# Two of eight token blocks by a dense pass over both expert tables, the other six by gathers

## Chip, cores and metric

The kernel runs on one core of a Trainium2 chip, all data in f32. The metric is the device time of one execution in microseconds. The median of three runs counts.

## What is computed

One layer of a decoder for 1024 prompt tokens and 32 sample tokens of width 1024. A token mixer comes first (adaLN, input projection, causal pooling and a convolution over 31 tokens, output projection). Then each token picks experts and adds their outputs:

```python
q = (hf @ w_query).reshape(-1, PEER_HEADS, 2, PEER_HALF)
s = jnp.einsum('nhpk,hpmk->nhpm', q, sub_keys)          # 8 heads, 2 x 128 keys
sv, si = lax.top_k(s, 16)
comb, cidx = ...                                         # 16 x 16 sums, i * 128 + j
fv, fpos = lax.top_k(comb, 16)
eid, gate = ..., jax.nn.softmax(fv)
a = jnp.einsum('phkd,pd->phk', u_table[ex], hx)          # 128 experts of 16384 a token
act = jax.nn.gelu(a) * gx
out = jnp.einsum('phk,phkd->pd', act, v_table[ex])
```

A last gated residual add and a final RMSNorm give the outputs. Both tables have 16384 rows of 4 KB, 67 MB each.

## The kernel before

The 1056 tokens form nine blocks: 0 to 7 of 128 prompt tokens, block 8 (SB) with the 32 sample tokens. For a block of 128 tokens the kernel fetches 128 "u tiles": tile k holds, on partition t, row `eid[t, k]` of u_table (GpSimd's indirect DMA in `u_fetch`, L807, 128 rows of 4 KB). VectorE multiplies it with h2 and sums over the row (L1381), which gives one dot per token. ScalarE applies Gelu (L965), VectorE the gate (`weigh`). Then it fetches 128 "v tiles": tile t holds the 128 rows of v_table that token t picked (`v_fetch`, L827), and TensorE multiplies it with the token's 128 weights into the accumulator banks 0 and 1 (`tokens`, L1758, four tokens in four groups of columns). `finish` adds the residual and norms a block. u tiles land in a ring of six places, v tiles in another of six.

Everything else is written into a table of slots. A slot is one pass of the loop over `p` (block) and `c` (NCH = 32 a block): four u tiles of block p, and from slot 17 on (V_LAG) four v tiles of the tokens 17 slots behind. Every engine walks the slots in order, and after its part of the gathers it does the steps that the slot lists. `lay_out` makes this table: `fill` puts the steps of the token mixer and of the query projection and scores for block groups 1 (blocks 2, 3, 4) and 2 (blocks 5, 6, 7, SB) one after another, each with a TensorE cost from COST, and goes to the next slot when the slot's load is over ROOM (7 for group 1, 4.6 for group 2, 9 in the first sixteen); `("gap", n)` moves on by n slots; two scores stand two slots apart. A score ("s", L1684) is followed by "best", VectorE's top 16 of four heads' keys in two halves (`key_tops`, L1270 to L1278). `spread` places the six pieces ("top", `piece`) by which VectorE makes the 16 x 16 sums, their top 16 and the expert numbers (L1294 to L1342). VectorE does a slot's steps one slot late (DVE_LAG). Group 0 (blocks 0 and 1) is done before slot 0, in the prologue. Weights come in tiles of 1 MB into two places of wring. The queue of SyncE loads and stores x, x1, h2 and y by a list `transfers` that is made from the slots. The steps stand in slots 5 to 184; the table has 288 slots, and the last 32 v tiles come behind it.

## Time and profile before

| | us |
|---|---|
| median of three runs | 3471.02 |
| lowest and highest | 3469.92, 3482.42 |
| span of the profiled execution | 3289.1 |
| TensorE busy | 2159.5 |
| VectorE busy | 2139.4 |
| GpSimd busy | 2280.5 |
| ScalarE busy | 368.6 |

The page gives no time of the profiled execution beside its span, which runs from the first to the last instruction; the runs' time holds what lies around it too. The mean granted clock of TensorE is 0.823 of full speed, 1235 MB are moved at a mean of 376 GB/s. A busy share says how long an engine had an instruction under way, with waits that lie inside an instruction's modelled duration.

### The profile page before, as it was taken

The page shows a single profiled execution, that of the slowest core. Times are in us where ns is not written, and L with a number is a line of the kernel's source. Part 1 is how long each engine was busy: PE and PEld are TensorE (multiplying, and loading weights), DVE is VectorE, ACT ScalarE, POOL GpSimd, SP SyncE. Part 2 cuts the span into 40 slices and gives each one's busy share as a digit, 9 for nine tenths or more (in the row PEclk, how much of TensorE's full clock was granted, in tenths as well). Part 3 has the DMA queues.
Part 4 walks back from the last instruction along what each step waited for, and adds up shares of the span by engine and source line. Part 5 has one row for each costly group of instructions (what it writes and reads, how often), then busy time and mean ns, then how long its engine had stood idle before and what let it go on. Part 6 is the DMA issues. An engine that isn't in the chain of part 4 may idle for free.

```text
span 3289.1 us, 30699 instructions
## 1 busy us (share of the span) xinstructions
PE 2159.5 (66%) x9831; PEld 958.8 (29%) x9831; DVE 2139.4 (65%) x4892; ACT 368.6 (11%) x793; POOL 2280.5 (69%) x2229
## 2 busy tenths in 40 slices
PE   6885896756776468997855577767454445545556
PEld 5573442212443113453211143434111111111111
DVE  1577756676788855666575657877766666677431
ACT  2112231100010110222100100001000000000000
POOL 0144677776777777777776777777777777777765
PEclk9997998977887789999877688889767777667679
DMA  8778899999999999999999999999999999999998
GB/s 290 202 273 299 326 385 386 388 401 401 397 395 389 360 396 406 405 405 386 382 400 394 375 399 390 392 382 370 369 405 406 402 402 406 406 385 402 382 363 321
DMA packets 363454, 1235.08 MB, mean 376 GB/s; under 512 B 36855, under 2 KB 40335, under 8 KB 363279
## 3 DMA queue, kind: packets, MB, share of 16 engines
q0 software_dynamic: 304784, 1109.40, 87.4%
q1 hardware_dynamic: 36335, 79.69, 6.8%
q10 hardware_dynamic: 22176, 44.04, 3.6%
q8 instruction: 79, 1.29, 0.2%
q14 instruction: 80, 0.66, 0.1%
HBM read 1220.31 MB, written 13.28 MB: 375 GB/s over the span
## 4 chain that ended last, share of the span: by engine, by line
POOL 29%; DMA 27%; PE 24%; issue 11%; DVE 7%; DVEq 1%; ACT 1%; SPq 0%; POOLq 0%; ACTq 0%
DMA v_ring<-in_v_table_dram,eidt 21%; POOL u_ring L807 15%; POOL v_ring L827 14%; PE bank L1758 13%; DMA u_ring<-in_u_table_dram,eid 4%; PE bank L1586 3%; PE bank L1668 2%; DVE u_ring L1381 2%; PE bank L1569 2%; PE bank L1644 2%; DMA u_ring<-in_v_table_dram,eidt 1%; DVE mixt L1211 1%; DVE work L1272 0%; DMA u_ring<-in_w_ada_dram 0%; POOL u_ring L827 0%
## 5 line engine op out<-in xcount | busy, mean ns | idle before, releaser
L1758 PE MATMUL bank<-v_ring,act_x 128*32 128x512 f32 x4104 | 1177.7, 808 | 977.7 <-DMA v_ring<-in_v_table_dram,eidt 929.9
L1381 DVE CUSTOM_DVE_ANT_0 u_ring<-u_ring,h 128x1024 f32<-128x1024 f32 x1056 | 1279.5, 1226 | 785.4 <-DMA u_ring<-in_u_table_dram,eid 711.9
L807 POOL DMA_INDIRECT u_ring<-in_u_table_dram,eid x1024 | 1129.9, 1103 | 444.0 <-issue 312.2
L827 POOL DMA_INDIRECT v_ring<-in_v_table_dram,eidt x1026 | 1070.3, 1043 | 397.3 <-issue 245.8
L1758 PEld LDWEIGHTS bank<-v_ring,act_x 128*32 128x32 f32 x4104 | 271.4, 135 | 1794.3 <-issue 1785.0
L1668 PEld LDWEIGHTS bank<-hbuf,wring 128*128 128x128 f32 x1984 | 228.4, 194 | 22.0 <-issue 22.0
L1668 PE MATMUL bank<-hbuf,wring 128*128 128x128 f32 (+1 forms) x1984 | 234.4, 279 | 0.0
L1586 PE MATMUL bank<-zc,dring 128*128 128x384 f32 x496 | 193.3, 514 | 4.0 <-ACT dring L860 4.0
L1569 PE MATMUL bank<-hbuf,wring 128*128 128x384 f32 (+2 forms) x448 | 150.8, 495 | 22.7 <-DMA wring<-in_w_in_dram 13.7
L1644 PE MATMUL bank<-wring,mixt 128*128 128x512 f32 (+1 forms) x256 | 123.2, 631 | 0.0
L1569 PEld LDWEIGHTS bank<-hbuf,wring 128*128 128x128 f32 x448 | 85.7, 194 | 89.7 <-issue 50.8
L1586 PEld LDWEIGHTS bank<-zc,dring 128*128 128x128 f32 x496 | 84.3, 192 | 58.0 <-issue 21.6
L860 ACT ACTIVATE dring<-ident,cw 128x128 f32<-128x128 f32 x248 | 78.1, 389 | 124.6 <-PE bank L1588 75.0
L1381 DVE DVE_READ_ACCUMULATOR2_ANT dot<- 128x1 f32 x1056 | 87.0, 82 | 0.0
L1409 DVE TENSOR_TENSOR scratch<-bank,mod 128x512 f32<-128x512 f32 x18 | 11.6, 686 | 102.1 <-PE bank L1758 100.8
L965 ACT ACTIVATE dot<-dot 128x32 f32<-128x32 f32 x33 | 7.6, 229 | 627.5 <-DVE dot L1381 627.4
L1644 PEld LDWEIGHTS bank<-wring,mixt 128*128 128x128 f32 (+1 forms) x256 | 46.7, 190 | 77.5 <-issue 77.5
L955 ACT ACT_TABLE_LOAD x34 | 43.6, 1283 | 144.4 <-PE bank L1644 95.5
L944 ACT ACTIVATE qt<-bank 128x512 f32<-128x512 f32 (+1 forms) x36 | 20.2, 561 | 350.1 <-PE bank L1668 350.1
L1588 PEld LDWEIGHTS bank<-zcs,dring 128*128 128x128 f32 x248 | 46.9, 189 | 33.0
L786 POOL DMA_DIRECT2D hbuf<-in_b_out_dram x1 | 0.7, 696 | 79.0 <-PE bank L1569 79.0
L1301 DVE TENSOR_TENSOR work<-fhalff,iota 128x512 f32<-128x512 f32 x72 | 49.8, 692 | 7.6 <-issue 0.7
(267 smaller groups left out, 1696.6 us busy)
## 6 DMA issues: line engine op xcount, KB each, us to landing
v_ring<-in_v_table_dram,eidt POOLq DMA_INDIRECT x1026, 6.9
u_ring<-in_u_table_dram,eid POOLq DMA_INDIRECT x1024, 6.8
wring<-in_w_out_dram ACTq DMA_DIRECT2D x16, 1024.0 KB, 11.9
wring<-in_w_query_dram ACTq DMA_DIRECT2D x16, 1024.0 KB, 11.7
wring<-in_w_in_dram ACTq DMA_DIRECT2D x10, 1024.0 KB, 11.8
xr<-in_x_prompt_dram SPq DMA_DIRECT2D x16, 512.0 KB, 7.4
v_ring<-in_w_ada_dram SPq DMA_DIRECT2D x7, 1024.0 KB, 13.4
wring<-in_w_ada_dram SPq DMA_DIRECT2D x5, 1024.0 KB, 5.6
```

The source lines that it names most:

```text
L807: pool.indirect_dma_start(u_ring[:, n % NU], None, u_table[0], bass.IndirectOffsetOnAxis(ap=col, axis=0)).then_inc(u_in[n % NU], 16)
L827: pool.indirect_dma_start(place, None, v_table[0], bass.IndirectOffsetOnAxis(ap=eidt[:, b % RING, t:t + 1], axis=0)).then_inc(landed, 16)
L860: last = act.activation(diag_at(g, c, j), ident[:, :], ACT.Copy, scale=cw[:, j, c:c + 1])
L955: act.activation(g, g, ACT.Exp).then_inc(exp_ready, 1)
L1301: dve.tensor_tensor(hot[:, :, :, :], fhalff[:, :, a * K:(a + 1) * K].unsqueeze(3).broadcast_to(shape), iota[:, :].unsqueeze(1).unsqueeze(1 ...
L1381: dve.tensor_tensor_reduce(u_ring[:, n % NU], u_ring[:, n % NU], h2[:, b % 2], 1.0, 0.0, ALU.mult, ALU.add, dot[:, b % 2, k:k + 1]).then_i ...
L1569: last = pe.matmul(ps[PROJ[c]][:, 0:n], w[:, k, c * P:(c + 1) * P], h1t[:, h * HK + k, 0:n], start=(h + k == 0), stop=(h * HK + k == KC - 1))
L1586: last = pe.matmul(ps[2 + c % 2][:, 0:np], diag_at(g, c, j), zc[:, c, j:j + np], start=(j == 0), stop=(j == CK - 1))
L1588: last = pe.matmul(ps[7][:, c * S:(c + 1) * S], diag_at(g, c, j), zcs[:, c, :, j:j + TS], start=(j == 0), stop=(j == CK - 1))
L1644: last = pe.matmul(bank, mixt[:, h * HK + k, t0:t0 + n], w[:, k, :], start=False, stop=(h * HK + k == KC - 1))
L1668: last = pe.matmul(q_bank(b)[:, a * n:(a + 1) * n], w[:, k, a * P:(a + 1) * P], h2_cols(b)[:, h * HK + k, :], start=(h + a + k == 0), stop ...
L1758: last = pe.matmul(acc[h][j * S:(j + 1) * S, :], act_x[:, i % 2, j, a:a + S], v_place(n)[0][:, h * HALF:(h + 1) * HALF], start=(c == 0), s ...
```

## The change

Blocks 2 and 3 no longer gather. Seven positions (POS: blocks 0, 1, 4, 5, 6, 7, SB) go through the slots, so the table has 224 slots. For the pair (2, 3), 256 tokens, the selection keeps the two key numbers and the gate of each pick (`dn`), and three new kinds of step follow in the slots.

- "numbers" and "unit": TensorE turns gates and key numbers. For four tokens at a time VectorE makes the first keys' one-hot times gate (`first_keys`: four comparisons over 128 columns), ScalarE the second keys' one-hot (`second_keys`: four Abs over 128 columns and one Relu over 512), TensorE multiplies them into a 128 x 128 gate matrix per token, ScalarE copies 512 columns out, and SyncE stores 16 tokens at a time in pieces of 512 bytes to `g_dram` (16.8 MB in all).
- "round" m: table tile m of u (128 experts, 512 KB) is turned by eight transposes, tile m - 3 is multiplied with the 256 tokens' h2 (eight products of 256 columns), ScalarE applies Gelu, VectorE multiplies with the gates loaded from `g_dram`, and four products of 512 columns with tile m - 6 of v add to banks 2 to 5. There are 134 rounds with 128 of each kind of work (130 transposed tiles, two of them h2 itself).
- two more ends (`finish`) for the dense blocks.

The new planner gives more room a slot (12 and 13), gaps are shorter, scores stand one slot apart, and VectorE does "best" in the slot of the score. The planner's text gives: mixer, query and score steps in slots 5 to 97; units six a slot in slots 98 to 108; rounds two a slot in 109 to 175, one round after each pair of tokens; gathers alone from 176. The v ring has five places, the sixth holds `dn` and constants. Tiles of u and v of the tables are loaded by SyncE's queue, three and five rounds ahead, into places that the mixer used. DVE, ACT and PE do a slot's dense steps between their parts of the gathers.

```diff
@@ -41,7 +41,7 @@
...
-NV = 6
+NV = 5
...
 PASSES = [[bs[i:i + 2] for i in range(0, len(bs), 2)] for bs in GROUPS]
-ROOM = [None, 7, 4.6]
+ROOM = [None, 12, 13]
+POS = [0, 1, 4, 5, 6, 7, SB]
+NPP = len(POS) - 1
+POS_OF = {b: p for p, b in enumerate(POS)}
+NSLOT = (NPP + 1) * NCH
+DENSE = [[2, 3]]
+DENSE_OF = {b: (r, q) for r, bs in enumerate(DENSE) for q, b in enumerate(bs)}
+NDB = 2
+DT = NDB * P
+NTILE = NKEY + NDB
+W_LAG = 4
+VD_LAG = 6
+NROUND = NKEY + VD_LAG
+UNIT = 4
+NUNIT = DT // UNIT
+STOK = 16
+NSTAGE = DT // STOK
+IC = 8
+NCHUNK = NKEY // IC
+NUD, NVD, NGE = 4, 6, 4
 MAXP = 3 * P
@@ -177,7 +196,7 @@
                 at = max(at, last + i[1])
                 continue
             if i[0] == "s":
-                at = max(at, scored.get("last", 0) + 2)
+                at = max(at, scored.get("last", 0) + 1)
             while load[at] >= (9 if at < LAG else room):
@@ -187,9 +206,9 @@
...
-                scored["last"], scored[i[1:]] = at, at + 1
+                scored["last"], scored[i[1:]] = at, at
                 for h in range(2):
-                    slots[at + h].append(("best", *i[1:], h))
+                    slots[at].append(("best", *i[1:], h))
         return at
@@ -224,9 +243,48 @@
...
-    for b in range(1, NB + 1):
-        last = spread(top_steps([(part, b) for part in range(PARTS)]), max(last, 24 + 30 * (b - 1)), min(24 + 30 * b, NB * NCH - 3))
+    for b, (s0, s1) in TOP_SLOTS.items():
...
+TOP_SLOTS = {1: (20, 30), 2: (36, 47), 3: (47, 57), 4: (55, 72), 5: (80, 96), 6: (98, 122), 7: (122, 152), SB: (152, NSLOT - NCH - 4)}
+GEN_UNITS, ROUNDS = (6,), (2,)
+
...
+def lay_out_dense(steps):
+
+    slots = [[] for _ in range(NSLOT)]
+    pieces = {"exp", "nrm", "top", "turn", "turned"}
+    at = max(s for s, todo in enumerate(steps) if any(x[0] not in pieces for x in todo)) + 2
+    ends = []
+    for r, bs in enumerate(DENSE):
+        at = max(at, max(s for s, todo in enumerate(steps) if ("nrm", PARTS - 1, bs[-1]) in todo) + 2)
+        slots[at] += [("numbers", r, q) for q in range(NDB)]
+        for u in range(NUNIT):
+            slots[at + u // GEN_UNITS[r]].append(("unit", r, u))
+        at += (NUNIT - 1) // GEN_UNITS[r] + 1
+        slots[at].append(("last", r))
+        for m in range(NROUND):
+            slots[at + m // ROUNDS[r]].append(("round", r, m))
+        at += (NROUND - 1) // ROUNDS[r] + 1
+        ends.append(at)
+    return slots, ends
+
+
...
+    g_dram = [nc.dram_tensor(f"gates_scratch{r}", [NDB, NCHUNK, P, P // STOK, IC, STOK], F32, kind="Internal").ap() for r in range(len(DENSE))]
...
+        gij = mflat[:, 0:6 * P].rearrange("p (q x t) -> p q x t", q=NDB, x=3)
...
+        zcf, zpf, zcsf = (z.rearrange(r) for z, r in ((zc[:, :, :], "p g n -> p (g n)"), (zp[:, :, :], "p g n -> p (g n)"),
+                                                      (zcs[:, :, :, :], "p g b n -> p (g b n)")))
+        oh_i, oh_j = (z[:, 0:2 * UNIT * P].rearrange("p (r t e) -> p r t e", r=2, t=UNIT) for z in (zcf, zpf))
+        ht = keyt[:, :, :].rearrange("p a m -> p (a m)").rearrange("p (k t) -> p k t", k=KC)
+        ut = [hbuf[:, i * D:(i + 1) * D] for i in range(2)]
+        ge = hbuf[:, 2 * D:3 * D].rearrange("p (r t) -> p r t", r=NGE)
+        gch = [wring[:, i].rearrange("p k n -> p (k n)").rearrange("p (b t i c) -> p b t i c", b=NDB, t=P // STOK, i=IC) for i in range(2)]
+        ud = [xr[:, 0], xr[:, 1], gt1[:, :], qt[:, :, :, :].rearrange("p i a n -> p (i a n)")]
+        vd = [mod2[:, 0], mod2[:, 1], dring[:, :, :].rearrange("p i k -> p (i k)"), zcf[:, 0:D], zpf[:, 0:D], zcsf[:, 0:D]]
         act_x = sb("act_x", [P, 2, 4, XW])
@@ -610,20 +718,101 @@
...
+            def stage_store(r, k):
+
+                n = r * NSTAGE + k
+                sp.wait_ge(unit_taken, (n + 1) * (STOK // UNIT))
+                q, t = divmod(k, P // STOK)
+                sp.dma_start(g_dram[r][q, :, :, t].rearrange("c j i t -> j c (i t)"),
+                             stage[n % 2].rearrange("p (c i) t -> p c (i t)", i=IC)).then_inc(g_stored[n % 2], 16)
...
+            def ud_load(r, t):
+
+                n = r * NTILE + t
+                if n >= NUD:
+                    sp.wait_ge(ut_ps, 2 * (n - NUD) + 2)
...
+                    sp.wait_ge(h2_stored[b % 2], 16 * (b // 2))
+                    src = h2_dram[b]
+                else:
+                    src = u_table[0, (t - NDB) * P:(t - NDB + 1) * P, :]
...
+            def vd_load(r, i):
+
+                n = r * NKEY + i
+                if n >= NVD:
...
+                    sp.wait_ge(st_ps, 4)
+                sp.dma_start(vd[n % NVD], v_table[0, i * P:(i + 1) * P, :]).then_inc(vd_in[n % NVD], 16)
...
+            def g_load(r, c):
+
+                n = r * NCHUNK + c
+                if n >= 2:
+                    sp.wait_ge(wd_ready, IC * (n - 1))
...
+                        sp.wait_ge(g_stored[a], 16 * NSTAGE // 2 * (r + 1))
+                sp.dma_start(gch[n % 2].rearrange("p b t i c -> p b (t i c)"),
+                             g_dram[r][:, c].rearrange("b j t i c -> j b (t i c)")).then_inc(g_in[n % 2], 16)
@@ -992,6 +1185,81 @@
...
+            def second_keys(r, u):
...
+                    act.wait_ge(unit_ps, n - 1)
+                for i in range(UNIT):
+                    act.activation(oh_j[:, n % 2, i], iota_e, ACT.Abs, bias=gij[:, q, 2, t + i:t + i + 1])
+                if u:
+                    unit_out(r, u - 1)
+                act.drain()
+                act.activation(oh_j[:, n % 2], oh_j[:, n % 2], ACT.Relu, bias=one_c, scale=-1.0).then_inc(oh_j_ready, 1)
...
+            def unit_out(r, u):
...
+                act.activation(stage[k % 2][:, :, i * UNIT:(i + 1) * UNIT].rearrange("p i t -> p t i"),
+                               ps[2 + n % 4][:, :].rearrange("p (t i) -> p t i", t=UNIT), ACT.Copy).then_inc(unit_taken, 1)
...
+            def dense_round(r, m):
+
+                if m < NTILE:
+                    n = r * NTILE + m
+                    for h in range(2):
+                        act.wait_ge(ut_ps, 2 * n + h + 1)
...
+                        to = ht[:, 4 * h:4 * h + 4, m * P:(m + 1) * P] if m < NDB else ut[m % 2][:, h * HALF:(h + 1) * HALF].rearrange("p (a t) -> p a t", a=4)
+                        act.activation(to, ps[7][:, :].rearrange("p (a t) -> p a t", a=4), ACT.Copy).then_inc(ut_ready, 1)
...
+                if 0 <= i < NKEY:
+                    n = r * NKEY + i
+                    act.wait_ge(a_ps, n + 1)
+                    if n >= NGE:
+                        act.wait_ge(vd_ps, NDB * (n - NGE + 1))
+                    act.activation(ge[:, n % NGE], ps[6][:, DT:2 * DT], ACT.Gelu).then_inc(ge_ready, 1)
@@ -1370,20 +1649,58 @@
...
+            def first_keys(r, u):
...
+                    dve.wait_ge(unit_ps, n - 1)
+                for i in range(UNIT):
+                    last = dve.tensor_scalar(oh_i[:, n % 2, i], iota_e, gij[:, q, 1, t + i:t + i + 1], gij[:, q, 0, t + i:t + i + 1],
+                                             ALU.is_equal, ALU.mult)
+                last.then_inc(oh_i_ready, 1)
...
+            def dense_weights(r, m):
...
+                    n, c = r * NKEY + i, r * NCHUNK + i // IC
+                    dve.wait_ge(ge_ready, n + 1)
+                    if i % IC == 0:
+                        dve.wait_ge(g_in[c % 2], 16 * (c // 2 + 1))
+                    w = ge[:, n % NGE].rearrange("p (a t) -> p a t", t=STOK)
+                    dve.tensor_tensor(w, w, gch[c % 2].rearrange("p b t i c -> p (b t) i c")[:, :, i % IC], ALU.mult).then_inc(wd_ready, 1)
@@ -1453,12 +1785,18 @@
...
                 for c in range(NCH):
-                    if p < NB or c < NSG:
-                        chunk(p, c)
-                    slot = p * NCH + c - DVE_LAG
-                    for step in steps[slot] if slot >= 0 else []:
+                    todo = dense[p * NCH + c]
+                    for end in ends[p * NCH + c]:
+                        finish(end)
+                    for j in range(CH):
+                        if p < NPP or c < NSG:
+                            dots(p, c, j, j + 1)
@@ -1725,29 +2064,115 @@
...
+            def unit(r, u):
...
+                for i in range(UNIT):
+                    last = pe.matmul(ps[2 + n % 4][:, i * P:(i + 1) * P], oh_j[:, n % 2, i], oh_i[:, n % 2, i], start=True, stop=True)
+                last.then_inc(unit_ps, 1)
...
+            def tile_turned(n, h):
...
+                for a in range(4):
+                    last = pe.transpose(ps[7][:, a * P:(a + 1) * P], ud[n % NUD][:, (4 * h + a) * P:(4 * h + a + 1) * P], ident[:, :])
+                last.then_inc(ut_ps, 1)
...
+            def dense_values(r, i, q):
...
+                    pe.wait_ge(vd_in[n % NVD], 16 * (n // NVD + 1))
+                    pe.wait_ge(wd_ready, n + 1)
...
+                for h in range(2):
+                    last = pe.matmul(ps[2 + 2 * q + h][:, :], ge[:, n % NGE, q * P:(q + 1) * P], vd[n % NVD][:, h * HALF:(h + 1) * HALF],
+                                     start=(i == 0), stop=(i == NKEY - 1))
+                last.then_inc(vd_ps, 1)
...
+            def dense_dots(r, i, s):
...
+                    pe.wait_ge(ge_ready, n)
+                for k in range(KC):
+                    last = pe.matmul(ps[6][:, DT:2 * DT], ut[i % 2][:, k * P:(k + 1) * P], ht[:, k, :], start=(k == 0), stop=(k == KC - 1))
+                last.then_inc(a_ps, 1)
...
+            def dense_round(r, m, s):
+
+                for h in range(2):
+                    if m < NTILE:
+                        tile_turned(r * NTILE + m, h)
+                    if 0 <= m - VD_LAG < NKEY:
+                        dense_values(r, m - VD_LAG, h)
+                if 0 <= m - NDB - 1 < NKEY:
+                    dense_dots(r, m - NDB - 1, s)
@@ -1814,15 +2239,22 @@
...
+                        weights(NPP, 0, p * NCH + c)
                     if v_chunk(p * NCH + c):
                         b, vc = v_chunk(p * NCH + c)
                         if vc % LAG == 0:
-                            weights(b, vc // LAG)
-                        tokens(b, vc)
-                    if p == NB and c == NSG + 2:
-                        weights(NB, 0)
+                            weights(b, vc // LAG, p * NCH + c)
+                        tokens(b, vc, (0,))
+                        for step in todo[:len(todo) // 2]:
+                            dense_step(p * NCH + c, *step)
+                        tokens(b, vc, (2,))
```

## Rows read from the trace of the kernel before

**Rows 1.** The page's span, busy times and transfer rate in 40 slices of the span

```profile
span 3289.1 us, 30699 instructions
...
PE 2159.5 (66%) x9831; PEld 958.8 (29%) x9831; DVE 2139.4 (65%) x4892; ACT 368.6 (11%) x793; POOL 2280.5 (69%) x2229
...
GB/s 290 202 273 299 326 385 386 388 401 401 397 395 389 360 396 406 405 405 386 382 400 394 375 399 390 392 382 370 369 405 406 402 402 406 406 385 402 382 363 321
```

**Rows 2.** The page's chain that ended last, by line

```profile
DMA v_ring<-in_v_table_dram,eidt 21%; POOL u_ring L807 15%; POOL v_ring L827 14%; PE bank L1758 13%; DMA u_ring<-in_u_table_dram,eid 4%; PE bank L1586 3%; PE bank L1668 2%; DVE u_ring L1381 2%; PE bank L1569 2%; PE bank L1644 2%; DMA u_ring<-in_v_table_dram,eidt 1%; DVE mixt L1211 1%; DVE work L1272 0%; DMA u_ring<-in_w_ada_dram 0%; POOL u_ring L827 0%
```

**Rows 3.** The page's costliest groups: busy, mean ns of one, idle before and its releaser

```profile
L1758 PE MATMUL bank<-v_ring,act_x 128*32 128x512 f32 x4104 | 1177.7, 808 | 977.7 <-DMA v_ring<-in_v_table_dram,eidt 929.9
L1381 DVE CUSTOM_DVE_ANT_0 u_ring<-u_ring,h 128x1024 f32<-128x1024 f32 x1056 | 1279.5, 1226 | 785.4 <-DMA u_ring<-in_u_table_dram,eid 711.9
```

**Rows 4.** TensorE's timeline near the end: start, duration, one pair of tokens a line

```profile
3208.98 1.91 PE L1758 MATMUL bank<-u_ring,act_x 128*32 128x512 f32 x8 [0.66 <-DMA u_ring<-in_v_table_dram,eidt]
3211.54 1.91 PE L1758 MATMUL bank<-v_ring,act_x 128*32 128x512 f32 x8 [0.65 <-DMA v_ring<-in_v_table_dram,eidt]
```

**Rows 5.** GpSimd's timeline, two gathers in a row

```profile
1337.71 0.93 POOL L807 DMA_INDIRECT u_ring<-in_u_table_dram,eid  x1 [0.30 <-issue]
...
1338.95 0.94 POOL L827 DMA_INDIRECT v_ring<-in_v_table_dram,eidt  x1 [0.30 <-issue]
```

**Rows 6.** Windows: us, busy of PE, PEld, DVE, ACT, POOL, then clock, DMA share, GB/s

```profile
204.90:1329.00 1124.10, 784.23 (x3536) 379.57 (x3536) 804.64 (x1954) 156.53 (x340) 801.56 (x718) 0.85 0.99 380
1329.00:2322.20 993.20, 714.81 (x3398) 338.73 (x3398) 684.56 (x1595) 125.26 (x278) 746.97 (x687) 0.85 1.00 389
2322.20:3079.00 756.80, 384.13 (x1212) 89.93 (x1206) 506.46 (x1043) 39.86 (x68) 572.65 (x570) 0.71 1.02 400
3079.00:3289.10 210.10, 116.29 (x425) 27.67 (x423) 56.11 (x98) 4.43 (x13) 132.48 (x134) 0.84 0.92 346
```

**Rows 7.** Window of slots 0 to 183, the dots' line alone

```profile
204.90:2322.20 2117.30, 892.10 (x1472) 0.85 1.00 384
```

**Rows 8.** VectorE's timeline, two key selections begin

```profile
1960.18 0.29 DVE L1270 MAX8 s_mem<-dring 128x8 f32<-128x128 f32 x1
...
1962.04 0.29 DVE L1270 MAX8 s_mem<-dring 128x8 f32<-128x128 f32 x1
```

**Rows 9.** VectorE's groups by form

```profile
L1304 DVE TENSOR_TENSOR work<-work,sif 128x512 f32<-128x512 f32 x72 | 50.1, 696 | 5.7 <-issue 0.4
...
L1275 DVE MAX8 fv<-work 128x8 f32<-128x256 f32 x72 | 30.8, 428 | 5.3
...
L1144 DVE TENSOR_SCALAR xr<-xr,sst 128x1024 f32<-128x1024 f32 x8 | 6.1, 762 | 0.6
```

**Rows 10.** ScalarE: four 128-column activations in the timeline, and a copy's group

```profile
1482.67 1.28 ACT L860 ACTIVATE dring<-ident,cw 128x128 f32<-128x128 f32 x4 [2.98 <-PE bank L1588]
...
L950 ACT ACTIVATE dring<-bank 128x512 f32<-128x512 f32 x28 | 16.7, 597 | 313.9 <-PE bank L1684 245.5 <-PE bank L1687 68.4
```

**Rows 11.** TensorE's timeline: bursts without waits, and one handover; records counted

```profile
59.47 13.98 PE L1569 MATMUL bank<-hbuf,wring 128*128 128x256 f32 x64
...
148.45 7.13 PE L1644 MATMUL bank<-v_ring,mixt 128*128 128x512 f32 x16
...
183.02 7.31 PE L1668 MATMUL bank<-hbuf,wring 128*128 128x128 f32 x64
191.01 1.16 PE L1684 MATMUL bank<-keyt,qt 128*128 128x128 f32 x8 [0.69 <-ACT qt L944]
...
717.97 1.97 PE L1654 MATMUL bank<-ident,xr 128*128 128x128 f32 x16
...
1509.39 1.94 PE L1758 MATMUL bank<-v_ring,act_x 128*32 128x512 f32 x16
```

**Rows 12.** DMA issues: count, KB each, median us to landing

```profile
wring<-in_w_in_dram ACTq DMA_DIRECT2D x10, 1024.0 KB, 11.8
...
mod_scratch<-y POOLq DMA_DIRECT2D x6, 64.0 KB, 6.4
```

447 lines of the change are left out of this document (338 added, 109 removed).

## Prediction

> **What bounds the kernel now.** I read the page from the top: span and busy shares, then the slices, the chain, the costliest groups, then windows cut at slot boundaries, then single bursts. No engine is busy over 69%, but the transfer rate stands near 400 GB/s in nearly every slice after the eighth [rows 1], and the chain that ended last goes through the gathers of v_ring and GpSimd's issues [rows 2]. TensorE's token product and VectorE's dots lie idle 930 and 712 us waiting for gathered tiles [rows 3]. So the kernel is bound by its 2112 gathers of 0.524 MB. Two details decide about the change. In steady state a pair of v tiles (1.05 MB) comes every 2.56 us [rows 4], 409 GB/s; and GpSimd needs about 1.24 us from issue to issue [rows 5], so the eight gathers of a slot take at least 9.9 us whatever the transfers do. Time taken off the transfers is no use beyond that.
>
> The profiled execution has a span of 3289.1 us, and the median of the runs is 3471.0 us, 181.9 us above it. I sum against the span and add the difference to the median. A measurement of this kernel can tell about 0.5% (17 us) from no change.
>
> **The plan before and after.** A slot is four u tiles and four v tiles. Slot 0 begins at 204.9 us; the before's slot 98 begins at 1328 and its slot 184, where the last mixer and query steps end, at 2322 us [rows 6]. From the planner's text, before: mixer and queries of groups 1 and 2 in slots 5 to 184. After: the same work in slots 5 to 97 (room 12 and 13 against 7 and 4.6, scores one slot apart, VectorE without its lag); slots 98 to 108 build the gate matrix (64 units, six a slot); slots 109 to 175 hold the 134 dense rounds, two a slot; then gathers alone. So there are five stages.
>
> **Prologue, 205 us.** Nothing of it is changed [rows 6].
>
> **Stage A, slots 0 to 97, forecast 1420 us.** Removed nothing, only packed. VectorE was busy 804.6 + 684.6 = 1489 us in the before's slots 0 to 183 [rows 6], 892 us of that in the dots [rows 7]: 1.212 us each for 736. The other 597 us now fall into 98 slots beside 392 dots (475 us): 1072 us busy. Small operations that follow on each other have gaps, which busy time leaves out; I allow a tenth, an estimate, so 597 becomes 657 and VectorE 1132 us. One key selection, gaps included, is 1.86 us from start to start [rows 8]. Transfers: 427.1 + 386.4 = 814 MB in that stretch [rows 6], less 86 slots of gathers (361 MB), is 453 MB, 1132 us at 400 GB/s. Two resources at 1132 us each would overlap perfectly only if both were even, and they are not. Slots 35 to 46 hold twelve scores (48 key selections, 89 us), 48 dots (58 us) and block 2's four parts of pair selection and key numbers: each has six operations over 512 columns at 0.69 us and twelve over 256 columns at 0.42 [rows 9], 9.2 us, 41 us for four with gaps; 188 us or 15.7 us a slot against 11.7 us of transfers. In slots 57 to 61 three convolution steps a slot do the same to TensorE. I priced every step of both plans in this way and took per slot the dearest of VectorE, TensorE and transfers. For the before's slots 0 to 183 that gives 2093 us against 2117 measured, so it may be trusted to some per cent. For the after's 0 to 97 it gives 1430 us; taking the dearest over eight slots together (as if the rings could average that far) it gives 1288 us. The rings hold six and five tiles, little over one slot, so I take 1420. Bounds: 1290, and 1560 if scores stall (below). The before needed 1124 us for these 98 slots [rows 6].
>
> **Stage B, slots 98 to 108, forecast 175 us.** ScalarE builds the second one-hot: per unit four 128x128 activations (1.28 us), one Relu over 128x512 and one 128x512 copy out of PSUM, 0.597 us each [rows 10], and a drain: 2.6 us, 64 times 166 us, plus the turn of the gates. VectorE's four comparisons over 128 columns lie between nothing and the 0.76 us of one over 1024 columns [rows 9]; I take 0.25, near the small end as 128 columns are an eighth of it, so 1 us a unit beside ScalarE. TensorE's four products, 0.228 us each [rows 11], are covered too. The gate matrix, 16.8 MB, is stored in 512-byte pieces. No row has such a store of 1 MB; 64 KB of 512-byte rows land in 6.4 us and 1 MB of 2 KB rows in 11.8 us [rows 12]. Sixteen stores at 11.8 us are 189 us, mostly under ScalarE's time: upper bound 200. The lower bound is the transfers alone, 88 gathers and the matrix, 63 MB, 155 us. The Trainium skill, DMA: Bandwidth & Descriptors, Specifications, puts the smallest transfer for line rate at 512 bytes; by it the store would cost no more than its bytes and the stage would end at ScalarE's 166 us. No row of this trace shows it.
>
> **Stage C, slots 109 to 175, forecast 1275 us.** Here the bound moves to TensorE. Per round it turns one u tile, multiplies it with 256 tokens and multiplies a v tile for two blocks: eight transposes, eight f32 products with 256 columns, four with 512. From back-to-back bursts [rows 11], where an f32 product is two records and a transpose is one: 32 products of 256 columns take 13.98 us (0.437 each), eight of 512 columns 7.13 us (0.89), sixteen transposes 1.97 us (0.123). A round is 3.50 + 3.56 + 0.98 = 8.04 us; less 0.1 us for the drains that end each burst 7.95 us, 128 rounds 1018 us. The token pairs of the gathered blocks are now issued in two halves with a round between them. Four tokens in one go take 1.94 us, a pair alone 1.91 [rows 4, 11], so splitting doubles their price: 134 x 1.91 = 256 us. Sum 1274 us, 19 us a slot. Beside it: transfers, 67 slots of 8 gathers, 4 dense tiles and an eighth of a 2.1 MB gate chunk, 6.55 MB or 16.4 us a slot at 400 GB/s, 1100 us; GpSimd 9.9 us; VectorE 4.85 us of dots, about 1 us of weights and up to 6 us of selections; ScalarE four copies at 0.6 and two Gelu, about 3.5 us. All are hidden by TensorE; if TensorE were free, transfers would be next at 1100. The lags (weights four rounds, values six) leave a round of slack, so the semaphores should cost little. Upper bound: one handover of 0.69 us [rows 11] in each round adds 88 us, with other work 1400. Lower: 1250, since a pair's 1.91 us holds the last product's drain. What the change buys here is the 536 gathers that pass meanwhile, which would take 714 us by themselves; it pays nearly as much again for the rest.
>
> **Stage D, slot 176 to the end, forecast 370 us.** 96 u and 164 v gathers are left. The last 210.1 us of the before [rows 6] moved 35 + 104 = 139; the other 121 are 63.4 MB, 159 us at 400 GB/s. Bounds 350 to 380. The dense blocks' own ends (four multiplications more on VectorE) hide under gathers.
>
> **Sum.** 205 + 1420 + 175 + 1275 + 370 = 3445 us, 156 above 3289, so 3471 + 156 = 3627; I say 3625 us. As a check by differences: 512 gathers saved are 64 slots of 10.66 us (756.8 over 71 plain slots [rows 6]), 682 us, and 86 slots are relieved of mixer work (11.55 to 10.66 us, 77 us); against this stage A is 296 us longer than before, stage B 58 above eleven plain slots, stage C 561 above 67 plain ones. The change moves 8% fewer bytes, but hands the bound to TensorE for 67 slots and to VectorE for much of the first 98.
>
> **Rivals.** *The packed stage averages out, and the change is faster.* If the rings absorb the peaks, stage A is 1290, B 165, C 1250 and D 355: 3265 us, a time of 3447. For it: the transfers alone would allow A in 1132. Against: the before's own slots 160 to 183, where VectorE's part is largest, follow the slot-by-slot sum and not the average. It decides where A and C together fall below 2540 us (forecast 2695). *No change*: the same, half as strong, with A near 1310 and C at 1275, about 3471 to 3515, a narrow case. *Scores stall.* VectorE now selects from a score in the slot in which TensorE makes it: query halves of 3.65 us (16 products at 0.228), two ScalarE copies and the score lie ahead of it, and VectorE's next dots, so GpSimd's next u gather, wait behind it. With 7 us lost in some 20 of the slots 35 to 46 and 80 to 96, A becomes 1560 and the time 3765. For it: the lag and gap that covered this are gone. Against: TensorE runs ahead of VectorE when VectorE is the late one. *Dense rounds starve*: if rounds wait for a table tile or a handover each, C is 1400 or more, time 3750. *The change does not do what it says*, for instance gathers run on and dense rounds trail behind: excluded by the order, each slot's pairs and rounds being written in one program order on TensorE.
>
> **How the numbers follow.** Forecast as summed, 3540 to 3700: 0.50. Scores stall 0.16, rounds starve 0.09: both slower. Faster rival 0.15. No change 0.10. So faster 0.15, same 0.10, slower 0.75. The range runs from 3440 (most of the faster rival and a tenth outside with the mishaps combined) to 3770, which takes in each single upper bound.
>
> **What would show it.** In the profile after: TensorE near full in the stretch of the dense rounds, at a granted clock near 1.0, with 16 dense records of 256 columns a round in about 3.5 us, and the transfer rate there below 360 GB/s; slots of about 19 us (dots per stretch). ScalarE near full for some 170 us before it. In the first 98 slots VectorE busy above 75% and the transfer rate below that of before. Slot 98 should begin near 1625 us, the rounds near 1800, and end near 3075. I am wrong if slot 98 begins by 1500, if the transfer rate stays at 400 in the dense stretch, or if a round takes less than 7.5 us of TensorE.

## The result, and the profile after

| | forecast | measured |
|---|---|---|
| time, median (kernel before beside it: 3470.5) | 3625 (3440 to 3770) | 3775.2 |
| ratio to the kernel before | 1.045 | 1.087, interval 1.083 to 1.091 |
| prologue | 205 | 206.0 |
| stage A, slots 0 to 97 | 1420 | 1607.8 |
| stage B, slots 98 to 108 | 175 | 254.9 |
| stage C, slots 109 to 175 | 1275 | 1295.9 |
| stage D, slot 176 to the end | 370 | 397.6 |

The kernel is slower, as forecast, but by 305 us instead of 154, and the time lies 5 us above the upper end of the range. The profiled execution has a span of 3762.2 us. The stages begin where the first dot of their first slot begins. Slower was right, stage C and the prologue were near (stage C 21 us over), A and B were not: they are 188 and 80 us longer than forecast.

The page of the changed kernel, busy tenths, clock and GB/s in 40 slices (94 us each), and its costliest groups:

```profile
span 3762.2 us, 38955 instructions
...
PE 2910.5 (77%) x13405; PEld 1627.7 (43%) x13405; DVE 1918.9 (51%) x4745; ACT 741.9 (20%) x1532; POOL 1812.7 (48%) x1717
...
PE   7868874665599765765566899999999999984456
...
DVE  2586577578744454677556343333343333346431
...
PEclk9988997887799887877677899999999999997778
DMA  8697688777975799776687998988989898879998
GB/s 282 178 346 248 218 320 306 290 265 257 331 262 186 247 367 354 274 256 219 237 267 252 372 350 321 362 327 332 339 327 350 328 342 332 329 284 380 370 346 314
...
PE bank L2183 12%; PE bank L2144 12%; PE bank L2131 11%; DMA v_ring<-in_v_table_dram,eidt 6%; PE bank L1922 5%; POOL u_ring L999 4%; PE bank L2004 4%; PE bank L2117 3%; POOL v_ring L1020 3%; DVE u_ring L1660 3%; PE bank L1905 3%; PE bank L2107 2%; PE bank L1980 2%; DMA u_ring<-in_u_table_dram,eid 2%
...
L2183 PE MATMUL bank<-v_ring,act_x 128*32 128x512 f32 x3080 | 819.1, 725 | 570.3 <-DMA v_ring<-in_v_table_dram,eidt 519.3
L1660 DVE CUSTOM_DVE_ANT_0 u_ring<-u_ring,h 128x1024 f32<-128x1024 f32 x800 | 950.5, 1223 | 249.0 <-DMA u_ring<-in_u_table_dram,eid 171.0
L2144 PE MATMUL bank<-keyt,hbuf 128*128 128x256 f32 x2048 | 465.8, 381 | 0.0
...
L2107 PE MATMUL bank<-zc,zp 128*128 128x128 f32 x512 | 98.4, 351 | 86.0 <-DVE zc L1675 63.1
```

Against [rows 1] the even 400 GB/s is gone. In slices 3 to 22, which are stages A and B, the rate lies mostly between 180 and 350, and no engine is near full in its place, but for TensorE in slices 12 and 13 (the convolution of blocks 5 to SB). In slices 24 to 35, stage C, TensorE is at 9 with the clock at 0.9 or more, and the rate lies near 340. The chain that ended last no longer goes mainly through gathers as in [rows 2]; its first three entries are products of TensorE. Windows at the stages' bounds, columns as in [rows 6]:

```profile
206.00:1813.80 1607.80, 1115.51 (x5560) 631.38 (x5560) 1045.19 (x2849) 251.61 (x566) 833.26 (x717) 0.84 0.78 280
1813.80:2068.70 254.90, 161.26 (x686) 95.28 (x686) 147.51 (x421) 189.53 (x390) 96.69 (x91) 0.73 0.76 252
2068.70:3364.60 1295.90, 1269.01 (x5206) 730.57 (x5207) 478.27 (x992) 243.34 (x452) 587.09 (x532) 0.99 0.89 335
3364.60:3762.20 397.60, 204.16 (x686) 47.34 (x684) 159.91 (x281) 14.90 (x30) 268.51 (x257) 0.78 0.95 353
```

In A VectorE was busy 1045 us (forecast 1072) and TensorE 1116 of 1608: the work is as counted, the overlap is not. VectorE's share is 65%, where the prediction wanted to see over 75%. In B no engine is busy over three quarters, though ScalarE should have been full. In C TensorE is at 98%.

**One thing about the baseline.** The kernel before took 3294 to 3298 us in two of the batches below and 3464 to 3486 in the others. Its profiled execution, with the span of 3289.1, is one of the first sort. A program's time is some 2 us above its span, so the 181.9 us that the prediction added to the span do not lie around it. What differs is the transfer rate. Slots 192 to 239 of the kernel before hold gathers and a few pieces of the selection, and so they do in p_room, a variant of it below: 10.47 us a slot at 404 GB/s in the first trace, 11.53 us at 366 GB/s in p_room's (windows: us, busy, clock, DMA share, GB/s):

```profile
2411.80:2914.40 502.60, 260.26 (x798) 60.41 (x796) 323.20 (x640) 25.17 (x44) 383.65 (x385) 0.71 1.02 404
```

```profile
2724.00:3277.70 553.70, 269.90 (x798) 58.70 (x796) 321.17 (x636) 23.77 (x42) 396.62 (x386) 0.71 0.97 366
```

The texts written ahead of the runs speak of a chip with 402 and one with 361 GB/s. The record has the same chip number (15) beside both rates; what sets the rate no run shows. Here the two are called the higher and the lower rate.

A kernel bound by transfers feels this, the changed one hardly: stages A to C of the changed kernel took 3159 us at the lower rate and 3141 at the higher one (b_act1, whose edit moved nothing). So the change's price depends on the rate: 8.7% at the lower one; at the higher one the variants b_act1 and b_dve1, both with the stages of the changed kernel, took 3742 and 3758, 13.5 and 14% above 3298. Below, each stage is compared at its own rate. b_ring3, b_act1, b_dve1, c_halfdots, c_unsplit, p_room and nodense ran once each.

### The profile page after: what moved, and what is told of

It reads as the page before. It is cut to its first block, busy times and chain, and to the rows that moved or that the text cites. A ratio compares the mean times of both kernels' runs of the same rounds, so it can differ in the third digit from the quotient of the medians.

```text
span 3762.2 us, 38955 instructions
## 1 busy us (share of the span) xinstructions
PE 2910.5 (77%) x13405; PEld 1627.7 (43%) x13405; DVE 1918.9 (51%) x4745; ACT 741.9 (20%) x1532; POOL 1812.7 (48%) x1717
## 4 chain that ended last, share of the span: by engine, by line
PE 57%; DVE 12%; DMA 10%; issue 8%; POOL 7%; ACT 2%; DVEq 2%; another core or an unknown queue 2%; SPq 0%; ACTq 0%; POOLq 0%
PE bank L2183 12%; PE bank L2144 12%; PE bank L2131 11%; DMA v_ring<-in_v_table_dram,eidt 6%; PE bank L1922 5%; POOL u_ring L999 4%; PE bank L2004 4%; PE bank L2117 3%; POOL v_ring L1020 3%; DVE u_ring L1660 3%; PE bank L1905 3%; PE bank L2107 2%; PE bank L1980 2%; DMA u_ring<-in_u_table_dram,eid 2%
## 5 line engine op out<-in xcount | busy, mean ns | idle before, releaser
L1020 POOL DMA_INDIRECT v_ring<-in_v_table_dram,eidt x770 | 836.7, 1087 | 994.4 <-PE bank L2183 804.2
L999 POOL DMA_INDIRECT u_ring<-in_u_table_dram,eid x768 | 893.9, 1164 | 785.5 <-DVE dot L1660 513.7
L2183 PE MATMUL bank<-v_ring,act_x 128*32 128x512 f32 x3080 | 819.1, 725 | 570.3 <-DMA v_ring<-in_v_table_dram,eidt 519.3
L1660 DVE CUSTOM_DVE_ANT_0 u_ring<-u_ring,h 128x1024 f32<-128x1024 f32 x800 | 950.5, 1223 | 249.0 <-DMA u_ring<-in_u_table_dram,eid 171.0
L2183 PEld LDWEIGHTS bank<-v_ring,act_x 128*32 128x32 f32 x3080 | 173.9, 125 | 1057.7 <-issue 1044.5
L2144 PE MATMUL bank<-keyt,hbuf 128*128 128x256 f32 x2048 | 465.8, 381 | 0.0
L2144 PEld LDWEIGHTS bank<-keyt,hbuf 128*128 128x128 f32 x2048 | 391.1, 191 | 106.9 <-issue 59.8
L1244 ACT ACTIVATE hbuf<-bank 128x512 f32<-128x512 f32 x256 | 152.9, 597 | 458.8 <-PE bank L2117 423.6
L1922 PE MATMUL bank<-zc,dring 128*128 128x384 f32 x496 | 202.9, 536 | 18.9 <-ACT dring L1053 16.8
L2131 PE MATMUL bank<-mod,hbuf 128*128 128x512 f32 x352 | 165.5, 593 | 0.0
L2107 PE MATMUL bank<-zc,zp 128*128 128x128 f32 x512 | 98.4, 351 | 86.0 <-DVE zc L1675 63.1
L1905 PE MATMUL bank<-hbuf,wring 128*128 128x384 f32 (+2 forms) x448 | 150.6, 498 | 16.8 <-DMA wring<-in_w_in_dram 12.6
L1675 DVE TENSOR_SCALAR zc<-v_ring,mixt 128x128 f32<-128x128 f32 x256 | 76.7, 370 | 102.3 <-PE bank L2107 79.3
```

What stands on the lines that cost most here:

```text
L999: pool.indirect_dma_start(u_ring[:, n % NU], None, u_table[0], bass.IndirectOffsetOnAxis(ap=col, axis=0)).then_inc(u_in[n % NU], 16)
L1020: pool.indirect_dma_start(place, None, v_table[0], bass.IndirectOffsetOnAxis(ap=eidt[:, b % RING, t:t + 1], axis=0)).then_inc(landed, 16)
L1660: dve.tensor_tensor_reduce(u_ring[:, n % NU], u_ring[:, n % NU], h2[:, b % 2], 1.0, 0.0, ALU.mult, ALU.add, dot[:, b % 2, k:k + 1]).then_i ...
L1905: last = pe.matmul(ps[PROJ[c]][:, 0:n], w[:, k, c * P:(c + 1) * P], h1t[:, h * HK + k, 0:n], start=(h + k == 0), stop=(h * HK + k == KC - 1))
L1922: last = pe.matmul(ps[2 + c % 2][:, 0:np], diag_at(g, c, j), zc[:, c, j:j + np], start=(j == 0), stop=(j == CK - 1))
L2107: last = pe.matmul(ps[2 + n % 4][:, i * P:(i + 1) * P], oh_j[:, n % 2, i], oh_i[:, n % 2, i], start=True, stop=True)
```

## Experiments

### What sets the first 98 slots

**a_lag**: VectorE does the steps of slots 0 to 96 one slot late, as the kernel before does.

```diff
+LAG_TO = 97
...
-                    for step in steps[p * NCH + c]:
+                    s = p * NCH + c
+                    for step in (steps[s - 1] if 0 < s <= LAG_TO else []) + (steps[s] if s >= LAG_TO else []):
```

> The changed kernel with VectorE doing the steps of slots 0 to 96 one slot late again; nothing else. Theory coupling (in stage A VectorE waits some 330 us for TensorE and ScalarE in the same slot, which the lag had covered): VectorE's waits on them fall below 100 us, slots 0 to 97 take 1430 to 1500 us against 1608, and the kernel 3600 to 3680. Rival (the stage is set by uneven work and small rings alone): stage A stays within 40 us of 1608.

3666.0 us, at the higher rate (3294.5 for the kernel before). Stage A took 1504.4 us, just above the expected 1430 to 1500; the five variants with A untouched took 1591 to 1598 at the same rate. The lag is worth 86 to 94 us (the texts written ahead of the later runs say 103, which compares two rates). VectorE's waits in stage A (source, us in total, times, longest), the changed kernel and then a_lag:

```profile
DVE u_ring L1660 <- DMA u_ring<-in_u_table_dram,eid: 113.8, 54, 11.9
DVE eidt L1639 <- PE bank L2039: 76.5, 5, 34.7
DVE s_mem L1540 <- ACT dring L1143: 37.2, 6, 12.5
DVE tops L1540 <- issue: 29.4, 3, 24.6
DVE fsum L1622 <- ACT gate L1148: 26.4, 2, 24.4
DVE mixt L1494 <- PE bank L1952: 23.9, 2, 20.4
```

```profile
DVE u_ring L1661 <- DMA u_ring<-in_u_table_dram,eid: 226.1, 75, 16.8
DVE eidt L1640 <- PE bank L2041: 45.3, 5, 16.8
DVE zc L1448 <- PE bank L1907: 27.4, 6, 11.2
```

All waits of VectorE except those for gathers fall together from 361 to 138 us (the kernel before: 25 us over slots 0 to 183); those with TensorE or ScalarE as the releaser are 269 and 119 of it. The waits for gathers rise from 114 to 226. VectorE waited for TensorE's turned numbers, for scores and for sums in the very slot in which they are made. How such a wait or a long selection travels, from the changed kernel's timeline (start, duration, idle before and its releaser):

```profile
716.67 0.30 DVE L1540 MAX8 tops<-dring 128x8 f32<-128x128 f32 x1 [24.56 <-issue]
...
724.29 1.23 DVE L1660 CUSTOM_DVE_ANT_0 u_ring<-u_ring,h 128x1024 f32<-128x1024 f32 x1 [0.21 <-issue]
...
725.79 1.68 POOL L999 DMA_INDIRECT u_ring<-in_u_table_dram,eid  x1 [9.47 <-DVE dot L1660]
...
730.07 0.94 POOL L1020 DMA_INDIRECT v_ring<-in_v_table_dram,eidt  x1 [0.30 <-issue]
...
737.60 5.13 PE L2183 MATMUL bank<-v_ring,act_x 128*32 128x512 f32 x16 [15.38 <-DMA v_ring<-in_v_table_dram,eidt]
```

VectorE had stood 24.6 us until a score was there (ScalarE's copy of it ends at 716.6; the profile names no releaser) and then made selections until 724. GpSimd stood 9.5 us at a u gather until a dot freed its place; the v gathers queued behind it started after 730; TensorE idled 15.4 us for them, from 722.2 on, and was then late with its own steps, for which VectorE waits next. The places of the v ring had been free since TensorE's last product of tokens, which ended at 721.1, so some 8 of the 15.4 us passed before the first v gather was issued at all. Over slots 0 to 97 GpSimd stood 405.9 us at u gathers for VectorE's dots, with the lag 235.9, in the kernel before 56.1; TensorE stood 350.0, 257.3 and 259.9 us for v tiles.

**a_mix**: a_lag, and GpSimd issues one u and one v gather in turn.

```diff
                             u_fetch(p, c * CH + j)
-                    if v_chunk(p * NCH + c):
-                        b, vc = v_chunk(p * NCH + c)
-                        for j in range(CH):
+                        if v_chunk(p * NCH + c):
+                            b, vc = v_chunk(p * NCH + c)
                             v_fetch(b, vc * CH + j)
```

> a_lag, and GpSimd issues a slot's gathers in turn, one of u and one of v, instead of four and four. If GpSimd's one queue is the link that still costs (a u gather that waits for VectorE holds back v gathers whose places are free, and the other way round), the first 98 slots fall from 1504 by 20 to 60 us. If the slot-by-slot sum of busy work is what is left, they stay within 10 us.

3729.8 us beside 3486.0; stage A 1562.8 us against 1518.8 for mended2, whose stage A is a_lag's, at the same rate: 44 us longer instead of 20 to 60 shorter. So the order in GpSimd's queue does matter, but this order is worse, and it is not the remedy. Why was not settled; one reading is that a v gather in front of the second u gather can stop the queue for TensorE as well.

**p_room**: the kernel before with the new planner's room alone (longer gaps, lag, six v places and scores two apart stay).

```diff
-ROOM = [None, 7, 4.6]
+ROOM = [None, 12, 13]
```

> The kernel before with only the planner's room changed to 12 and 13, gaps and lag as they were; all eight blocks gather. Theory (packing mixer work costs time of its own, since slots then fall to VectorE or TensorE and the gathers' lead is lost): the kernel is slower than before by 60 to 150 us although nothing is added. Rival (packing is free, the later slots give back what the first lose): within 25 us of before.

3676.4 us beside 3463.8: 213 us, 6.1%, for packing and nothing else, far above the expected 60 to 150. This kernel has no dense work, moves the same bytes and keeps the lag; its mixer and query steps end in slot 147 instead of 184. The late slots do not pay the loss back: slots 152 to 239 took 11.46 us each, the time of their gathers at this rate (slots 192 to 239 have a DMA share of 0.97, above), whatever their engines do not have to do. Where the loss arises is seen best in the sixteen convolution steps of blocks 5 to SB. They stand one a slot in the kernel before (slots 99 to 114) and three a slot here (82 to 87). Windows of these slots in the kernel before and in p_room:

```profile
1341.40:1510.50 169.10, 161.97 (x750) 88.08 (x750) 116.05 (x219) 51.24 (x149) 130.66 (x127) 1.00 1.02 404
```

```profile
1260.00:1379.20 119.20, 114.77 (x510) 70.71 (x509) 42.50 (x78) 35.70 (x109) 48.47 (x48) 0.98 0.66 234
```

One a slot, TensorE (96% busy) and the transfers (404 GB/s) work side by side. Three a slot, TensorE is as full (96%), but the transfers stand at 234 GB/s, and the gathers of ten slots are still to come, 115 us. 119 + 115 is 234 us for what would take some 187 at this rate (169.1 us, at 366 instead of 404 GB/s; an estimate). The work is the same, but it has less beside it.

**nodense**: the changed kernel without numbers, units and rounds (blocks 2 and 3 get no experts).

```diff
-        slots[at] += [("numbers", r, q) for q in range(NDB)]
-        for u in range(NUNIT):
-            slots[at + u // GEN_UNITS[r]].append(("unit", r, u))
...
-        for m in range(NROUND):
-            slots[at + m // ROUNDS[r]].append(("round", r, m))
```

The ends of blocks 2 and 3 wait for the scores and the state here instead of the rounds.

> The gate matrix and all dense rounds are left out, so the outputs of blocks 2 and 3 lack their experts. Theory (stage A does not depend on them, the rest is what the dense pass costs): slots 0 to 97 stay at 1590 to 1610, slots 98 to 175 fall from 1551 to 78 plain slots of about 10.7, 835, and the kernel to about 3030. Rival (the smaller v ring slows plain slots too): slots 98 to 175 take over 880.

3124.2 us; A 1607.3 (unchanged: nothing of the dense part reaches into A), slots 98 to 108 125.7 and 109 to 175 781.8. Together that is 907.5 us, in the range that the text gave to its rival, the smaller v ring. But this batch ran at the lower rate: 78 slots at the 11.5 us of p_room, which has six v places, are 897, so some 10 us at most are left for the ring here. In the changed kernel of the same batch (a0_after) the two stretches are 256.3 and 1300.2: the dense pass costs 131 + 518 = 649 us. It replaces 64 slots of 11.5 us, 736 us, at this rate. By this estimate it gains 87 us by itself; packing the mixer's work ahead of it costs more.

**a0_after** is the changed kernel in that batch.

> The changed kernel, unchanged, beside before on one chip. In the run before this batch the kernel before took 3294 us and not 3471, with the same trace as the one first shown. Theory (the two chips differ in what transfers cost, and only the transfer-bound kernel feels it): if before takes about 3294 here, the changed kernel takes 3740 to 3765, nearly as on the other chip, ratio 1.135 to 1.145. Rival (both scale alike): about 3580, ratio 1.087.

3771.0 us beside 3463.8, ratio 1.088 (1.081 to 1.096): the first result again. This batch ran at the lower rate too, so it could not decide between the two theories; b_act1 and b_dve1, at the higher rate, did: 13.5 and 14% above the kernel before, as the first theory says.

**b0_before** is the kernel before in the batch of a_lag.

> The kernel before, unchanged, for a trace of the same chip as the others. Its profiled span was 3289 us while its runs took 3471. Theory 1 (the shown trace was an execution with quicker transfers than the timed ones): the span is now 3460 to 3480, the prologue about 205, and the missing 180 us are spread over the slots, about 11.9 us a plain slot against 10.66. Theory 2 (some constant lies outside the span): the span is again near 3290.

3295.0 us, span 3286.2, ratio 1.000: its slots follow the first trace's within 3 us.

### What sets a unit's 4 us

**b_ring3**: three one-hot buffers in place of two (`n % 2` becomes `n % 3` for `oh_i` and `oh_j`, and both engines wait for unit n - 3 only).

> Three one-hot buffers instead of two. Theory (the units are slow because VectorE and TensorE hand two buffers back and forth, 79 and 63 us of waits): slots 98 to 108 fall from 255 to 200 to 215. Rival (VectorE's and TensorE's own work in a slot and the token pairs between the units set it): they fall by less than 15 us.

Stage B 253.0 us against 256.3, time 3777.7: no effect.

**b_gen4**: `GEN_UNITS = (4,)` in place of 6.

> The gate matrix is built four units a slot: 16 slots (98 to 113) in place of 11, everything else the same, the rounds begin five slots later. If a unit has a price of its own (about 4 us from one to the next, a chain over ScalarE, VectorE and TensorE), the units end after the same 255 us with five more slots of gathers in them, the last stage is shorter by five plain slots, and the time falls by about 55 us. If slots and units add up (11.5 us a slot and 1.95 us a unit), the 16 slots take 16 x 11.5 + 64 x 1.95 = 309 us and the time stays within 10 us.

Slots 98 to 113 took 258.4 us and the time is 3698.0, 44 us below b_act1 of the same batch. The 64 units have a price of their own, 4.0 us each with the turn of the gates ahead of them, whether 11 or 16 slots of gathers pass beside them.

**b_act1** and **b_dve1**: one operation over 512 columns in place of four over 128, on ScalarE and on VectorE (three of four tokens' numbers are left out).

```diff
-                for i in range(UNIT):
-                    act.activation(oh_j[:, n % 2, i], iota_e, ACT.Abs, bias=gij[:, q, 2, t + i:t + i + 1])
+                act.activation(oh_j[:, n % 2], iota_e.unsqueeze(1).broadcast_to([P, UNIT, P]), ACT.Abs, bias=gij[:, q, 2, t:t + 1])
```

> Slots 98 to 108 with ScalarE's four Abs over 128 columns a unit (1.28 us) made one over 512 columns (about 0.6 us): the key numbers of three of four tokens are left out of the second one-hot. If ScalarE sets the unit's pace, as predicted, the stage falls by up to 64 x 0.7 = 45 us, from 255 to 210. If VectorE's order (comparisons of 1.48 us a unit between its dots, and the dots behind them) sets it, the stage stays within 10 us of 255.

> Slots 98 to 108 with VectorE's four comparisons over 128 columns a unit (1.48 us) made one over 512 columns (about 0.7 us): the key numbers and gates of three of four tokens are left out of the first one-hot. If VectorE is in the loop that sets the pace (comparison, product, copy, and the dots that wait behind them), the stage falls by 30 to 50 us, from 255 to 205 to 225. If ScalarE alone sets it, it stays within 10 us of 255.

Stage B 254.6 and 253.0 us. Neither the Abs nor the comparisons are on the path. The stores hardly are either: in b_act1 a 1 MB store in 512-byte rows lands in 9 us, and one is due every 16:

```profile
gates_scratch<-mixt SPq DMA_DIRECT2D x8, 1024.0 KB, 9.4
gates_scratch<-mod SPq DMA_DIRECT2D x8, 1024.0 KB, 8.7
```

Buffers, Abs and comparisons were out by a run, the stores by their times. The timeline of the changed kernel showed what was left, two units of it:

```profile
1906.29 1.11 DVE L1675 TENSOR_SCALAR zc<-v_ring,mixt 128x128 f32<-128x128 f32 x4 [1.15 <-PE bank L2107]
...
1907.39 0.72 ACT L1216 ACTIVATE zp<-zp,v_ring 128x512 f32<-128x512 f32 x1
1908.02 1.26 ACT L1212 ACTIVATE zp<-v_ring,mixt 128x128 f32<-128x128 f32 x4
...
1908.22 2.04 PE L2107 MATMUL bank<-zc,zp 128*128 128x128 f32 x8 [1.97 <-DVE zc L1675]
...
1910.30 1.04 ACT L1227 ACTIVATE mod<-bank 128x512 f32<-128x512 f32 x1 [1.01 <-PE bank L2107]
...
1911.42 0.72 ACT L1216 ACTIVATE zp<-zp,v_ring 128x512 f32<-128x512 f32 x1
```

The Relu (L1216) ends at 1908.1 and the product begins 0.1 us later. The profile names VectorE's comparison (L1675) as the product's releaser, but that one had ended at 1907.40; in all 64 units of this trace it ends before the Relu does. The product's end releases the copy (L1227); and in ScalarE's program the next Relu stands behind that copy, 4.03 us after the last one. The mean over the 64 units is 3.79 us. The Abs (L1212) lies in the loop's shadow, as does VectorE.

**b_order**: the copy goes behind the next Relu.

```diff
-                if u:
-                    unit_out(r, u - 1)
                 act.drain()
                 act.activation(oh_j[:, n % 2], oh_j[:, n % 2], ACT.Relu, bias=one_c, scale=-1.0).then_inc(oh_j_ready, 1)
+                if u:
+                    unit_out(r, u - 1)
```

> ScalarE copies a unit's product out of PSUM after its next Relu instead of before it. Theory (one loop through all three engines): in the trace a Relu (0.72 us) releases TensorE's four products (1.13 us at full clock, 2.04 at the lower one), these release the copy (1.03 us), and the next Relu stands behind that copy on ScalarE, 3.1 to 4.0 us a unit, whatever the buffers and the Abs; with the copy behind the Relu the loop is open and ScalarE's own 1.26 + 0.72 + 1.03 = 3.0 us a unit is left: the stage falls from 255 to about 200 us, the time from 3742 to about 3690 (chip with 402 GB/s). Rival (transfers of the gate matrix in 512-byte pieces, or the waits for v tiles in TensorE's order, set the pace): the stage stays within 10 us of 255.

Stage B fell from 256 to 202.3 us and the time to 3721.3, 50 below a0_after (beside 3486.0, ratio 1.065). The loop was the cause of these 54 us. Two Relus and what stands between, then the window of the stage:

```profile
1909.59 0.72 ACT L1214 ACTIVATE zp<-zp,v_ring 128x512 f32<-128x512 f32 x1
...
1910.22 1.06 ACT L1227 ACTIVATE mod<-bank 128x512 f32<-128x512 f32 x1
...
1911.08 1.23 ACT L1212 ACTIVATE zp<-v_ring,mixt 128x128 f32<-128x128 f32 x4
...
1912.38 0.72 ACT L1214 ACTIVATE zp<-zp,v_ring 128x512 f32<-128x512 f32 x1
```

```profile
1806.80:2009.10 202.30, 134.01 (x691) 80.87 (x692) 146.18 (x423) 177.53 (x391) 102.96 (x91) 0.87 0.93 315
```

Relu to Relu is 2.79 us here and 2.96 in the mean, ScalarE is busy 88% of the stage and the transfer rate is 315 GB/s instead of 252. This is the bound that the prediction had named, reached only after the edit, and at 202 us instead of 175: a unit takes 2.96 us, not 2.6, and the first Relu comes 14 us after the stage's begin.

### What sets the rounds

**c_halfdots**: the dense dots over four of the eight parts of the width.

```diff
-                for k in range(KC):
-                    last = pe.matmul(ps[6][:, DT:2 * DT], ut[i % 2][:, k * P:(k + 1) * P], ht[:, k, :], start=(k == 0), stop=(k == KC - 1))
+                for k in range(KC // 2):
+                    last = pe.matmul(ps[6][:, DT:2 * DT], ut[i % 2][:, k * P:(k + 1) * P], ht[:, k, :], start=(k == 0), stop=(k == KC // 2 - 1))
```

> The dense dots sum over four of the eight parts of the width, so half of that product is left out: 4 x 0.437 = 1.75 us less of TensorE a round. Theory TensorE-bound rounds: the dense stage falls from 1296 by 200 to 224 us, to 1075 to 1095, where transfers (1100 at 400 GB/s) begin to count, so 1100 is possible. Rival (semaphore handovers or table tiles set the round): it falls by less than 60 us.

**c_unsplit**: four tokens in one burst ahead of the rounds of a slot.

```diff
-                        tokens(b, vc, (0,))
+                        tokens(b, vc)
...
-                        tokens(b, vc, (2,))
```

> All four tokens of a slot in one go ahead of the two dense rounds instead of a pair ahead of each. Theory TensorE-bound, pair price: four tokens 1.94 us instead of 2 x 1.91, so the dense stage falls by up to 67 x 1.9 = 126 us, to about 1170. Rival: with a ring of five v tiles four tokens are not there in one go, TensorE waits for the last ones and the stage stays or grows.

3555.2 and 3662.9 us. Stage C fell from 1296 (b_act1, same rate) to 1105.9 and to 1206.5 us, by 190 and 90. TensorE's removed work is 128 x 4 x 0.437 = 224 and 67 x 1.88 = 126 us, so most of it comes straight off the stage. In c_unsplit the token product's busy time fell by 95 us (255.4 to 160.8): a burst of four tokens took 2.4 us on average and not 1.94, and waits for v tiles before it rose from 5.2 to 22.9 us, as its rival had it in small. The same edit made stage B 13 us longer (267.6), so the whole gain against b_act1 is 79 us. Window of the dense slots in c_halfdots:

```profile
2060.00:3160.00 1100.00, 1053.33 (x4170) 536.55 (x4163) 473.11 (x984) 241.99 (x450) 574.35 (x528) 0.98 1.00 393
```

The DMA share is 1.00 at 393 GB/s: the transfers are full now, at the 1100 us that the prediction gave for them. TensorE is still busy 96% of the time, so the two bounds lie close together.

### Put together

**mended** is a_lag, c_unsplit and b_gen4 in one; **mended2** adds b_order.

> Three things at once: VectorE does the steps of slots 0 to 96 one slot late, the four tokens before the rounds are one burst, and the gate matrix is built four units a slot (slots 98 to 113) instead of six. If the costs found so far add up: stage A 1504 us instead of 1608, the rounds 1210 instead of 1300; the slots of the units together with the plain slots after the rounds save another 0 to 50 us, so 3771 - 103 - 90 = 3578 us, less up to 50. Rival: the gains overlap (tokens late for the same reason) and the time stays above 3640. In no theory does it come below the kernel before (3464 to 3471 on a chip with 361 GB/s, 3294 on one with 402).

> mended with ScalarE's copy behind the next Relu. If the loop is the cause, slots 98 to 113 fall from 278 us to 200 to 220, and the time from 3522 to about 3450 to 3465 (kernel before 3298 on the chip of mended): still about 5% slower. If the transfers set the pace: 3520.

mended: 3522.0 us beside 3297.9, ratio 1.067 (1.064 to 1.071), 220 below b_act1 where the parts alone gave 76, 79 and 44: they add up, and a little more. mended2: 3506.0 beside 3486.0, ratio 1.007 (1.004 to 1.010), 265 us below a0_after. Its forecast was for the higher rate, and the batch ran at the lower one. Its 16 slots of units took 239.5 us, above the expected 220, at 361 GB/s and a DMA share of 0.98: the transfers hold that stage.

```profile
1723.60:1963.10 239.50, 159.62 (x790) 93.16 (x790) 178.18 (x496) 183.87 (x402) 153.33 (x132) 0.76 0.98 361
```

**m3** and **m5** stretch the packed work again. m3 is mended2 with group 2's scores two slots apart (mixer and queries end in slot 111); m5 gives group 2 a room of 9 instead of 13 as well (slot 117; its diff against mended2 follows, with VectorE's lag reaching to slot 118; in m3 the lag reaches to slot 111 and the pieces of blocks 5 and 6 are moved likewise).

```diff
-ROOM = [None, 12, 13]
+ROOM = [None, 12, 9]
...
-                at = max(at, scored.get("last", 0) + 1)
+                at = max(at, scored.get("last", 0) + (2 if i[2] >= GROUPS[2][0] else 1))
...
-TOP_SLOTS = {1: (20, 30), 2: (36, 47), 3: (47, 57), 4: (55, 72), 5: (80, 96), 6: (98, 122), 7: (122, 152), SB: (152, NSLOT - NCH - 4)}
+TOP_SLOTS = {1: (20, 30), 2: (36, 47), 3: (47, 57), 4: (55, 72), 5: (89, 119), 6: (121, 127), 7: (127, 152), SB: (152, NSLOT - NCH - 4)}
```

> mended2, and the scores of blocks 5, 6, 7 and SB two slots apart as in the kernel before: mixer and query steps end in slot 111 instead of 96, the gate matrix and the rounds come 15 slots later, the gathers alone at the end are 15 slots fewer. If peaks of VectorE within a slot cost the time (these 16 slots took 17 to 19 us each, against 10.7 or 11.5 us of transfers in a plain slot), the time falls by 40 to 80 us against mended2 (3506 us beside 3486 for the kernel before on a chip with 361 GB/s). Rival: the busy work only moves, and the time stays within 15 us.

> m3 with a room of 9 in place of 13 for the second group's mixer steps, which end in slot 117 instead of 96. Slots 56 to 61, where three convolution steps a slot took 20 us each, are relieved too. If packing is the cost: 60 to 110 us less than mended2, and faster than the kernel before by 1 to 2% on a chip with 361 GB/s, still slower by 2 to 4% on one with 402 GB/s. Rival: as for m3, within 15 us of mended2.

m3: 3507.6 beside 3483.4, ratio 1.006 (1.003 to 1.009): no gain. Its slots 80 to 97 took 253 instead of 309 us, but its slot 129 begins at 2131 us, where mended2's slot 114 (1963) and 15 plain slots (171) give 2134: with VectorE's lag in place the scores' time had only moved. m5: 3460.7, ratio 0.9925 (0.989 to 0.997), 45 us below mended2, less than the expected 60 to 110.

The convolution is one place where m5 gains. Its sixteen steps for blocks 5 to SB lie in slots 58 to 65, two a slot, instead of 56 to 61, three a slot. Windows of these slots in mended2 and in m5:

```profile
1016.40:1132.90 116.50, 110.52 (x498) 68.62 (x497) 57.76 (x124) 35.18 (x107) 45.87 (x45) 0.99 0.64 228
```

```profile
1030.10:1148.60 118.50, 116.01 (x562) 72.50 (x563) 70.99 (x152) 43.98 (x130) 67.81 (x64) 1.00 0.83 299
```

TensorE holds both, for 117 and 119 us, but in m5 the gathers of eight slots pass beside it instead of six, worth 23 us at 11.5. In all, m5's first 119 slots took 1662 us, where mended2's first 98 (1519) and 21 plain ones are 1760. Part of these 98 us is lost again behind them: the units took 271.8 us instead of 239.5. m5 is the only version below the kernel before, by 0.75%, clear of the noise but small, and at the lower transfer rate; at the higher one it was not run.

## Why the prediction was right and wrong

**Direction and stage C: right, by its own mechanism.** In stage C the bound went to TensorE for the dense slots. One round and a pair of tokens in the changed kernel:

```profile
2302.05 1.91 PE L2183 MATMUL bank<-v_ring,act_x 128*32 128x512 f32 x8
2303.89 0.66 PE L2117 MATMUL bank<-ident,xr 128*128 128x128 f32 x4
2304.39 1.88 PE L2131 MATMUL bank<-mod,hbuf 128*128 128x512 f32 x4
2306.11 0.60 PE L2117 MATMUL bank<-ident,xr 128*128 128x128 f32 x4
2306.54 1.88 PE L2131 MATMUL bank<-mod,hbuf 128*128 128x512 f32 x4
2308.26 3.62 PE L2144 MATMUL bank<-keyt,hbuf 128*128 128x256 f32 x16
2311.81 1.91 PE L2183 MATMUL bank<-v_ring,act_x 128*32 128x512 f32 x8
```

From pair to pair 9.76 us, forecast 7.95 + 1.91 = 9.86. The 0.1 us that the forecast took off for the ends of bursts is seen here: a burst begins 0.07 to 0.17 us before the end shown for the last one. The doubled price of the split pair is real (c_unsplit), and so is the second bound (c_halfdots). A gate chunk is 1 MB and not 2.1, but serves four slots, so the bytes a slot were right. "Dense rounds starve" did not happen: TensorE is busy 98% of the stage, at a granted clock of 0.99.

**Stage A: the step that failed is the slot-by-slot sum.** It took the dearest engine per slot, which supposes that nobody waits inside a slot for what another engine makes there. It gave 1420 us; the runs showed 1591 to 1598 at the rate that it was made for, and 1607.8 at the lower one. First, it put the removed lag at nothing, and a_lag shows that the lag is worth some 90 us. Slots 35 to 46, which the prediction priced at 188 us, took 246.0 in the changed kernel and 199.1 with the lag back. The prediction had this as a rival, "scores stall", at 140 us and a chance of 0.16. Its argument against, that TensorE runs ahead when VectorE is the late one, does not hold in the timeline shown: GpSimd's one queue made TensorE late behind VectorE. That this is the usual way of the loss is argued from that stretch and from GpSimd's 405.9 us of waits, and no run shows it alone. Second, 84 us remain above 1420 with the lag back (1504.4). Where they lie stays open, since the prediction gives the price of few slots. In a_lag's slots 57 to 61, the convolution, TensorE was busy 96.4 of 102.4 us, much as the sum says; in slots 81 to 96, the scores, VectorE, the busiest, was busy 214.0 of 246.7. The ring of five v places and the shorter gaps were not tested alone. a_mix shows only that the gathers' order counts. That the sum met the kernel before within 24 us was no proof: there the transfers were full on average (a DMA share of 0.99 and 1.00 [rows 6]), and waits between engines hide under them. And it was luck that the rival's time, 3765, lies near the 3775 measured: its 140 us are 90, and other misses make up for it.

**Stage B: the step that failed is "ScalarE-bound, 2.6 us a unit".** Each duration was near (1.26 against 1.28 for four Abs, 0.72 and 1.04 against 0.6 for Relu and copy), but the engines were summed one by one, and the order written for ScalarE closes a loop through two of them. The loop was to be read in `second_keys` before any run. The comparison of VectorE was also mis-sized (0.37 us against 0.25), without effect. The bounds of 155 to 200 missed. What the runs showed in its place is a loop of 3.79 us a unit over ScalarE and TensorE, and 2.96 us a unit once it is open (b_order). The store in 512-byte pieces cost no more than its bytes: in mended2's units, with all its stores among the gathers, the transfers ran at 361 GB/s, as fast as p_room's gathers alone at 366 within 2%. The Trainium skill, DMA: Bandwidth & Descriptors, Specifications, gives 512 bytes as the smallest transfer that reaches line rate, and the trace agrees.

**Stage D and the baseline.** D took 390 to 398 us at the higher rate and 398 to 405 at the lower; forecast 370. The term at fault is its transfer time: b_act1's slots 178 to 198 took 11.4 us each, where eight gathers at 400 GB/s make 10.5. Why they took longer is open. The sum of the stages, 3445, stands to about 3740 at the rate of the trace it was made from, 295 us too low. The 181.9 us added for the distance to the median were a change of the transfer rate, which only transfer-bound stretches feel. By luck they made the forecast look nearer (3625 to 3775) than its working was.

## What to carry to other kernels

Work that hides beside a full resource at one step a slot is no longer hidden at three a slot: spread it out, and count what passes beside it. A table that gave each slot the dearest engine was near the truth here only where one resource was dearest in nearly all slots; once several take turns, ask for each in-order queue what it holds back while it waits, and keep a slot of lag between the maker and the user. For a pipeline of small steps over several engines, follow one item around the engines in their written order before adding up busy times: if a copy of the last item stands before the next item's release, the loop is the sum, not the maximum. And when a kernel's trace and its timed runs differ by some per cent, find the stretch that differs before scaling anything.

## What the runs showed of the hardware that was not expected

The same gathers ran at 404 GB/s in some batches and at 366 in others, which moves a transfer-bound kernel by 5% (3295 to 3464 or more us) and the stages A to C of the changed one by under 1%. In stage B TensorE's clock went between its two levels: four 128-column products took 1.16 us at 1913 us, where the granted clock was 1.00 (2.4 GHz), and 2.04 us at 1908 us, where it was 0.50 (1.2 GHz). Its mean was 0.73 with the loop and 0.87 with the loop open (windows above), so the loop was longer by the clock too. ScalarE's copy out of PSUM into a place with a stride of 16 elements took 1.04 us over 512 columns, against 0.60 for those into rows without gaps (L1244 in the changed kernel, and [rows 10]); no run takes the stride alone away.
